# Four instead of three seven-product pairs of k-tiles in each gate/up chunk of a decoder layer

## The chip, the cores and the metric

The kernel runs on one core of a Trainium2 chip. Its time is the device time of one execution in microseconds; the median of three runs of the kernel before is 1977.46 us (1975.88 to 1978.14).

## What is computed

One decoder layer on 256 tokens of width 2048, in f32: a SwiGLU half-step, a mixing stage (a gated linear recurrence and a sparse attention behind one input projection), a cross attention on a memory of 256 tokens, a second SwiGLU half-step, and a last RMSNorm. The change touches only the two half-steps:

```
def swiglu(h, w_gate, w_up, w_down):
    return (jax.nn.silu(h @ w_gate) * (h @ w_up)) @ w_down
x = x + 0.5 * swiglu(rmsnorm(x, ffn_norm), w_gate, w_up, w_down)   # D = 2048, D_FF = 5632
```

## The kernel before, in words

**Matmuls in f32 from three passes.** Every f32 operand is split into a part hi, rounded to the type fp32r, and a rest lo. A product is three matmuls: hi by hi, hi by lo, lo by hi (`product`, L1886; `unit`, L1839). A weight unit is 512 KB. SP (the DMA queue of SyncE) loads it into one of four slots of `w_raw`; ScalarE (ACT) writes `w_hi` (L584); VectorE (DVE) writes `w_lo` = w_raw - w_hi (L1094); TensorE (PE) uses it. A load waits for the w_lo of the unit four before it (L462). w_hi of a unit waits until PE is done with the unit four before it (L583). DVE and ACT thus work four units ahead of PE (`split_ahead`, L685 and L1217: at position p they prepare the unit p + 4). Each engine takes its instructions in the order in which the program lists them.

**The gate/up stage** (`ffn_up` of each engine) makes the hidden values in 11 chunks of 512 columns. The first chunk (`opening`) is done in plain form, gate and then up, 8 units of two k-tiles each. The other ten are `body`, run as a hardware loop for chunks 1 to 9 and once more for chunk 10, with `ending` set. In a body a unit is one k-tile (128 of the 2048 rows) with 512 gate and 512 up columns, 16 units to a chunk. A plain unit (`both_unit`, L1898) makes four products, for two token halves by gate and up, into banks 0 to 3 of PSUM: 12 matmuls.

**A pair in seven-product form.** Two neighbouring units can be taken together as a product of 2 by 2 blocks with seven products instead of eight (`pair_units`, L1923): 21 matmuls instead of 24, four products in the first unit (banks 4, 6, 7, 5) and three in the second (banks 0, 1, 2). It needs sums of the blocks. The sums of tokens are made once per stage, in the opening (`token_forms` L1265, five instructions of DVE, then s_hi by ACT L715 and s_lo by DVE L1279), at the positions in FORMS_AT and FORMS_LO, in one buffer for each pair. The sums of weights are made anew in each chunk (`weight_sums`, L1235): a difference in place in w_raw (L1239), two more into `t_f32` (L1244, L1246), of which L1244 waits for both loads of the pair and, with `free_at`, until PE is done with the pair before; then t_hi by ACT (L700) and t_lo by DVE (L1229). All pairs share the one buffer t_f32, t_hi, t_lo. PAIR_AT gives the positions of the pairs in a chunk, PAIRS their k-tiles. Sums for the pair at 0 are made in the chunk before, at its position 12.

**Evictions of a chunk.** What the pairs gathered in banks 4 to 7 is added into `comb`: at MID_EV, the position of the last pair, ACT copies bank 4 (L762) and DVE adds bank 5 (L1339); at TURN_H, one position later, DVE adds banks 6 and 7 (L1343), and later bank 6 again (L1359). Also at TURN_H PE transposes the hidden values of the chunk before (`batch`, L1995, into bank 4 and 5), and ACT (L603) and DVE (L1127) split them into ffT. At position 14 DVE adds banks 0 to 3 (L1354, two instructions, behind the last unit of the chunk), ACT applies the Silu (L768), and DVE multiplies (L1288). PE begins the next chunk only when L1359 and L1127 are done (L1996, L1997).

**The down stage** (`ffn_down`) has six pairs of its own at DOWN_AT and uses the same buffers; its positions are not changed.

Of the kernel before, what the change touches and what calls it, by code (L numbers as in the profile page):

```python
# [5 lines left out]
P = 128  # L6
F32 = mybir.dt.float32
F32R = mybir.dt.float32r
# [8 lines left out]
SEQ = 256  # L17
NT = SEQ // P
# [29 lines left out]
KF = D_FF // P  # L48
# [6 lines left out]
              (C_NSA, NW), (C_NSA + NW, NW)]  # L55
             + [(c, NW) for c in (1024, 1536, 0, 512, 2048, 2560, 3072, 3584)])

PAIRS = ((0, 1), (2, 3), (4, 5))
PAIR_AT = (0, 6, 10)
W_KT = [0] * KD  # L60
for _i, _p in enumerate(PAIR_AT):
    W_KT[_p], W_KT[_p + 1] = PAIRS[_i]
_rest = [p for p in range(KD) if p not in PAIR_AT and p - 1 not in PAIR_AT]
for _kt, _p in enumerate(_rest):
    W_KT[_p] = 2 * len(PAIRS) + _kt
U_CH = KD
MID_EV = PAIR_AT[-1]
TURN_H = MID_EV + 1
NP = len(PAIRS)
DOWN_AT = (6, 12, 18, 24, 30, 36)  # L70
# [7 lines left out]
DOWN_EV = DOWN_AT[-1]  # L78
T_FFN, S_FFN = NP * (FF_CHUNKS - 1) + ND, NP + ND
EV_FFN = 3 * FF_CHUNKS + 2  # L80
FORMS_AT = ((3, 4, 11), (5, 7, 9))
FORMS_LO = ((5, 6, 14), (7, 9, 11))

U_GU1 = 0
U_DN1 = U_GU1 + 2 * U_G * FF_CHUNKS
# [65 lines left out]
def layer_program(nc, a, c, out):  # L151

    with ExitStack() as ctx:
# [8 lines left out]
        def put(name, shape, dt, size=4):  # L162
            n = size
            for s in shape[1:]:
                n *= s
            t = nc.alloc_sbuf_tensor_at(name, shape, dt, offset=at[0])
            at[0] += (n + 31) // 32 * 32
            return t
# [20 lines left out]
        s_hi = [nc.alloc_sbuf_tensor_at(f"s_hi{i}", [P, 4, P], F32R, offset=o) for i, o in enumerate(s_at)]  # L189
        s_f32 = [nc.alloc_sbuf_tensor_at(f"s_f32_{i}", [P, 4, P], F32, offset=o + 2048) for i, o in enumerate(s_at)]  # L190
        s_tmp = [nc.alloc_sbuf_tensor_at(f"s_tmp{i}", [P, 2, NT, P], F32, offset=o) for i, o in enumerate(s_at)]
        x_in = nc.alloc_sbuf_tensor_at("x_in", [P, NT, 2 * NW], F32, offset=at_xT[0])
        s_lo = [nc.alloc_sbuf_tensor_at(f"s_lo{i}", [P, 4, P], F32R, offset=o + 2048) for i, o in enumerate(s_at)]
# [26 lines left out]
        ff = at[0]  # L220
        ffT_hi = put("ffT_hi", [P, KF, SEQ], F32R)
        ffT_lo = put("ffT_lo", [P, KF, SEQ], F32R)
        ff_end = at[0]
        assert ff_end <= base + 206 * 1024, ff_end - base


# [343 lines left out]
        def _(act):  # L570
# [52 lines left out]
            def root(norm):  # L623
                act.wait_ge(var_ready, norm + 1)
                nc.scalar.activation(std[:, norm, :], var[:, norm, :], ACT.Sqrt).then_inc(std_ready, 1)
# [59 lines left out]
            def split_ahead(u0, ch, p, wide, opening=False):  # L685
# [3 lines left out]
                q = (p + SLOTS) % U_CH  # L689
                i = PAIR_AT.index(q) if q in PAIR_AT else PAIR_AT.index(q - 1) if q - 1 in PAIR_AT else None  # L690
                if not wide or i is None:
                    split(u, slot, turn_no)
                    return
                n_pair = (T_FFN if u0 else 0) + NP * ch + (1 - NP if p + SLOTS < U_CH else 1) + i
                if q in PAIR_AT:
                    act.wait_ge(t1_ready, n_pair)
# [16 lines left out]
            def token_hi(i, count):  # L713
                act.wait_ge(s_f32_ready, count)
                nc.scalar.activation(s_hi[i][:], s_f32[i][:], ACT.Copy).then_inc(s_hi_ready, 1)  # L715

            def ffn_up(u0, norm, b_h, b_x3, s_x3, base_c, base_x):
# [3 lines left out]
                def opening():  # L721
                    for k in range(2 if base_c else 0, 2 * U_G):
# [5 lines left out]
                        if not base_c and k == 10:  # L728
                            root(norm)
                        if k - 1 in FORMS_AT[u0 > 0]:  # L730
                            i = FORMS_AT[u0 > 0].index(k - 1)
                            token_hi(i, S_FFN * (u0 > 0) + i + 1)
# [349 lines left out]
        def _(dve):  # L1082
# [38 lines left out]
            def take(b, pos, lo, klo, hi, khi, scale=None):  # L1121
                dve.wait_ge(turn_hi, b + 1)
                if scale is None:
                    dyn = not isinstance(klo, int)
                    lo_v = lo[:, bass.ts(klo[0], 4), :] if dyn else lo[:, klo:klo + 4, :]
                    hi_v = hi[:, bass.ts(khi[0], 4), :] if dyn else hi[:, khi:khi + 4, :]
                    nc.vector.tensor_tensor(lo_v, turn[pos], hi_v.bitcast(F32), ALU.subtract).then_inc(turn_lo, 1)  # L1127
                    return
                for j in range(4):
                    last = nc.vector.scalar_tensor_tensor(  # L1130
                        out=lo[:, klo + j, :], in0=turn[pos][:, j, :], scalar=vec[:, scale + j:scale + j + 1],
                        in1=hi[:, khi + j, :].bitcast(F32), op0=ALU.mult, op1=ALU.subtract)
                last.then_inc(turn_lo, 1)
# [8 lines left out]
            def inverse(norm):  # L1142
                dve.wait_ge(std_ready, norm + 1)
                nc.vector.reciprocal(rstd[:, norm, :], std[:, norm, :]).then_inc(rstd_ready, 1)
                dve.wait_ge(rstd_ready, norm + 1)
# [8 lines left out]
            def split_x(j):  # L1154
                dve.wait_ge(xs_hi, j + 1)
                k = KT_U * j
                split_cols(xT_lo, k, xt_raw, k, xT_hi, k, V_F1 + k, xs_lo, KT_U)
# [59 lines left out]
            def split_ahead(u0, ch, p, wide, opening=False):  # L1217
# [3 lines left out]
                q = (p + SLOTS) % U_CH  # L1221
                i = PAIR_AT.index(q) if q in PAIR_AT else PAIR_AT.index(q - 1) if q - 1 in PAIR_AT else None
                if not wide or i is None:
# [52 lines left out]
            def token_lo(i, count):  # L1276

                dve.wait_ge(s_hi_ready, count)
                nc.vector.tensor_tensor(s_lo[i][:], s_f32[i][:], s_hi[i][:].bitcast(F32), ALU.subtract)\  # L1279
                  .then_inc(s_lo_ready, 1)  # L1280

            def ffn_up(u0, norm, b_h, b_x3, s_x3, base_c, sq):
# [3 lines left out]
                def products(up):  # L1286
                    for t in range(NT):
                        last = nc.vector.scalar_tensor_tensor(  # L1288
                            out=comb[:, 2 * t + 1, :], in0=up(t), scalar=rstd[:, norm, t:t + 1],
                            in1=comb[:, 2 * t, :], op0=ALU.mult, op1=ALU.mult)  # L1290
                    return last

                def opening():
                    for k in range(2 if base_c else 0, 2 * U_G):
                        if k == 4 and b_x3 is not None:
                            take(b_x3, 0, xT_lo, 12, xT_hi, 12, s_x3 + 12)
                        if not base_c and k < U_G - SLOTS:
                            split_x(SLOTS + k)
                        if not base_c and k == 11:
                            inverse(norm)  # L1300
                        if k == U_CH - 2:
                            dve.wait_ge(unit_done, u0 + U_CH)
                            dve.wait_ge(gate_ready, base_c + 1)
                            if b_h:
                                dve.wait_ge(turned, b_h)
                            last = products(lambda t: pair[1][:, t, :])
                            last.then_inc(h_ready, 1)
                            nc.vector.memset(taken_mark[:], 0.0).then_inc(c_taken, 2)
                        split_ahead(u0, 0, k, k + SLOTS >= U_CH, True)
                        if k in FORMS_LO[nth]:  # L1310
                            i = FORMS_LO[nth].index(k)
                            token_lo(i, S_FFN * nth + i + 1)
                        if not base_c and k in X_SQ:
                            n = X_SQ.index(k)
                            dve.wait_ge(x_loaded[n], 16)
                            link(nc.vector.scalar_tensor_tensor(
                                out=hb[:, 0, :], in0=x[:, 1, n * NW:(n + 1) * NW], scalar=1.0,
                                in1=x[:, 1, n * NW:(n + 1) * NW], op0=ALU.mult, op1=ALU.mult,
                                accum_out=ss[:, N_F1, 1, n:n + 1]))
                        if k in FORMS_AT[nth]:  # L1320
                            i = FORMS_AT[nth].index(k)
                            if i == NP - 1:
                                dve.wait_ge(sq_done, sq)
                                if base_c:
                                    dve.wait_ge(x_saved, 16)
                            if nth == 0:
                                dve.wait_ge(xs_lo, i + 1)
                            token_forms(i, PAIRS[i][0], xT_hi, xT_lo)
                        if k == (5 if base_c else 9):
                            variance(norm, sq)  # L1330
                        if base_c and k == 5:
                            inverse(norm)
# [505 lines left out]
        def _(pe):  # L1838
# [115 lines left out]
            def ffn_up(u0, b_x, b_h, b_x3, free_b, base_c):  # L1954
# [25 lines left out]
                def body(ch, ending):  # L1980
                    for p in range(U_CH):
                        u, slot = u0 + U_CH * ch + p, (u0 + p) % SLOTS
                        if p in PAIR_AT:
                            i = PAIR_AT.index(p)
                            pair_units(u, slot, i, PAIRS[i], tokens, S_FFN * nth + i + 1, T_FFN * nth + NP * (ch - 1) + i + 1,
                                       i == 0, i == NP - 1, 2 * base_c + 2 * ch if i == 0 else None)
# [520 lines left out]
```

## Time and profile before

| | |
|---|---|
| median of three runs | 1977.46 us |
| profiled execution | 1977.94 us |
| its span | 1976.1 us |
| PE busy | 1956.9 us, 99% |
| DVE busy | 1529.0 us, 77% |
| ACT busy | 1062.1 us, 54% |
| mean granted TensorE clock | 0.999 |

The span is the time from the first to the last instruction. A busy share is the mean over the whole span, with stages of different limits in it. The granted clock is a share of full speed. Durations of matmuls in the trace overlap, since they are pipelined; the distance of their starts is what one costs.

### The profile page before, as it was taken

The page shows a single profiled execution, that of the slowest core. Times are in us where ns is not written, and L with a number is a line of the kernel's source. Part 1 is how long each engine was busy: PE and PEld are TensorE (multiplying, and loading weights), DVE is VectorE, ACT ScalarE, POOL GpSimd, SP SyncE. Part 2 cuts the span into 40 slices and gives each one's busy share as a digit, 9 for nine tenths or more (in the row PEclk, how much of TensorE's full clock was granted, in tenths as well). Part 3 has the DMA queues.
Part 4 walks back from the last instruction along what each step waited for, and adds up shares of the span by engine and source line. Part 5 has one row for each costly group of instructions (what it writes and reads, how often), then busy time and mean ns, then how long its engine had stood idle before and what let it go on. Part 6 is the DMA issues. An engine that isn't in the chain of part 4 may idle for free.

```text
span 1976.1 us, 27433 instructions
## 1 busy us (share of the span) xinstructions
PE 1956.9 (99%) x10022; PEld 1616.1 (82%) x10022; DVE 1529.0 (77%) x1906; ACT 1062.1 (54%) x1305; POOL 13.6 (1%) x19
## 2 busy tenths in 40 slices
PE   9999999999999999999999999999999999999998
PEld 7888888888888888878777888888888888888886
DVE  7898899998886456766658675689999989888544
ACT  6555555555555444455555564555555555555443
POOL 0000000000000000000002000000000000000000
PEclk9999999999999999999999999999999999999999
DMA  9566666567766657565443465566666666666764
GB/s 300 184 202 199 202 193 209 183 201 235 228 222 193 194 165 220 176 198 157 137 124 114 163 202 169 160 227 207 193 191 209 187 200 205 203 208 202 247 192 147
DMA packets 148546, 382.69 MB, mean 194 GB/s; under 512 B 13424, under 2 KB 19824, under 8 KB 148080
## 3 DMA queue, kind: packets, MB, share of 16 engines
q1 hardware_dynamic: 146368, 378.70, 60.6%
q10 hardware_dynamic: 2096, 2.87, 0.4%
q8 instruction: 55, 0.90, 0.2%
q14 instruction: 27, 0.22, 0.0%
HBM read 377.33 MB, written 4.19 MB: 193 GB/s over the span
## 4 chain that ended last, share of the span: by engine, by line
PE 96%; ACT 1%; DMA 1%; DVE 1%; issue 0%; SPq 0%; DVEq 0%; ACTq 0%
PE psum L1889 54%; PE psum L1853 36%; PE psum L1876 2%; PE psum L2160 1%; PE psum L2203 1%; PE psum L1865 1%; DMA w_raw<-in_gu 0%; PE psum L2258 0%; ACT prob L886 0%; DMA w_raw<-in_w_in 0%; PE psum L2173 0%; DVE w_lo L1094 0%; ACT w_hi L584 0%; PE psum L2182 0%; ACT silu_gate L886 0%
## 5 line engine op out<-in xcount | busy, mean ns | idle before, releaser
L584 ACT ACTIVATE w_hi<-w_raw 128x1024 fp32r<-128x1024 f32 x694 | 725.7, 1056 | 674.3 <-PE psum L1853 324.7
L1094 DVE TENSOR_TENSOR w_lo<-w_raw,w_hi 128x1024 fp32r<-128x1024 f32 x694 | 835.7, 1221 | 310.1 <-ACT w_hi L584 307.9
L1889 PE MATMUL psum<-w_hi,xT_hi 128*128 128x512 f32 x920 | 360.2, 391 | 0.0
L1889 PE MATMUL psum<-w_hi,xT_lo 128*128 128x512 f32 x920 | 358.4, 390 | 0.0
L1889 PE MATMUL psum<-w_lo,xT_hi 128*128 128x512 f32 x920 | 358.3, 389 | 0.0
L1853 PE MATMUL psum<-w_hi,xT_hi 128*128 128x512 f32 (+1 forms) x544 | 213.0, 392 | 3.0 <-DVE w_lo L1211 2.8
L1853 PE MATMUL psum<-w_hi,xT_lo 128*128 128x512 f32 (+1 forms) x544 | 209.4, 385 | 0.0
L1853 PE MATMUL psum<-w_lo,xT_hi 128*128 128x512 f32 (+1 forms) x544 | 209.2, 385 | 0.0
L1889 PEld LDWEIGHTS psum<-w_hi,xT_lo 128*128 128x128 f32 x920 | 172.7, 188 | 36.1
L1889 PEld LDWEIGHTS psum<-w_lo,xT_hi 128*128 128x128 f32 x920 | 172.9, 188 | 35.1
L1889 PEld LDWEIGHTS psum<-w_hi,xT_hi 128*128 128x128 f32 x920 | 172.8, 188 | 35.1
L1853 PE MATMUL psum<-w_hi,ffT_hi 128*128 128x512 f32 x432 | 169.4, 392 | 0.0
L1853 PE MATMUL psum<-w_hi,ffT_lo 128*128 128x512 f32 x432 | 168.4, 390 | 0.0
L1853 PE MATMUL psum<-w_lo,ffT_hi 128*128 128x512 f32 x432 | 168.2, 389 | 0.0
L700 ACT ACTIVATE t_hi<-t_f 128x1536 fp32r<-128x1536 f32 x60 | 89.5, 1491 | 93.6 <-DVE t_f L1246 93.6
L1229 DVE TENSOR_TENSOR t_lo<-t_f,t_hi 128x1536 fp32r<-128x1536 f32 x60 | 105.5, 1759 | 25.3 <-ACT t_hi L700 25.3
L1853 PEld LDWEIGHTS psum<-w_hi,xT_hi 128*128 128x128 f32 x544 | 102.2, 188 | 24.1 <-DVE w_lo L1211 2.9
L1853 PEld LDWEIGHTS psum<-w_hi,xT_lo 128*128 128x128 f32 x544 | 102.1, 188 | 20.4
L1853 PEld LDWEIGHTS psum<-w_lo,xT_hi 128*128 128x128 f32 x544 | 102.4, 188 | 18.8
L1889 PE MATMUL psum<-w_hi,ffT_hi 128*128 128x512 f32 x280 | 109.5, 391 | 0.0
L1889 PE MATMUL psum<-w_lo,ffT_hi 128*128 128x512 f32 x280 | 109.1, 390 | 0.0
L1889 PE MATMUL psum<-w_hi,ffT_lo 128*128 128x512 f32 x280 | 109.1, 390 | 0.0
(319 smaller groups left out, 2508.3 us busy)
## 6 DMA issues: line engine op xcount, KB each, us to landing
w_raw<-in_gu SPq DMA_DIRECT2D x351, 512.0 KB, 4.3
w_raw<-in_d SPq DMA_DIRECT2D x176, 512.0 KB, 4.6
w_raw<-in_w_in SPq DMA_DIRECT2D x88, 512.0 KB, 3.8
w_raw<-in_w_out SPq DMA_DIRECT2D x32, 512.0 KB, 3.8
w_raw<-in_cw SPq DMA_DIRECT2D x8, 512.0 KB, 4.0
w_raw<-in_wk SPq DMA_DIRECT2D x8, 512.0 KB, 4.5
w_raw<-in_wq SPq DMA_DIRECT2D x8, 512.0 KB, 3.7
w_raw<-in_wv SPq DMA_DIRECT2D x8, 512.0 KB, 3.6
```

Source lines behind the costliest of these rows:

```text
L584: nc.scalar.activation(w_hi[:, slot], w_raw[:, slot], ACT.Copy).then_inc(w_hi_ready, 1)
L700: nc.scalar.activation(t_hi[:], t_f32[:], ACT.Copy).then_inc(t_hi_ready, 1)
L1094: nc.vector.tensor_tensor(w_lo[:, slot], w_raw[:, slot], w_hi[:, slot].bitcast(F32), ALU.subtract)\
L1229: nc.vector.tensor_tensor(t_lo[:], t_f32[:], t_hi[:].bitcast(F32), ALU.subtract).then_inc(t_lo_ready, 1)
L1853: mm = nc.tensor.matmul(dst[:, t, 0:width], act_t, w[:, slot, kk, 0:width], start=(first and kk == 0 and n == 0), stop=(last and kk == KT_ ...
L1865: mm = nc.tensor.matmul(dst[:, t, :], act_t, w[:, u % SLOTS, kk, :], start=False, stop=(last and kk == KT_U - 1 and n == 2))
L1876: tr = nc.tensor.transpose(turn[pos][:, j, t * P:(t + 1) * P], src(j, t), ident[:])
L1889: mm = nc.tensor.matmul(psum[:, bank, :], act_t, w, start=(first and n == 0), stop=(last and n == 2))
L2160: mm = nc.tensor.matmul(psum[:, 4 + hh, b * w:(b + 1) * w], qT[r, h // 2, t * P:(t + 1) * P], kT[r, b, h // REP, 0:w], start=True, stop=True)
L2203: mm = nc.tensor.matmul(psum[hh * DH:(hh + 1) * DH, 7, (r // 2) * P:(r // 2 + 1) * P], z_n[:, kk, c0:c0 + DH], probT[:, hh, (b * nk + kk) ...
```

## The change

There are four pairs, of k-tiles 0 to 7, at positions 0, 4, 8 and 12 of a chunk of 16, instead of three at 0, 6 and 10. Since MID_EV is the last pair's position, it goes from 10 to 12 and TURN_H from 11 to 13. The order of the k-tiles in a chunk (W_KT) and the count of pairs (NP) follow. A fourth buffer for the sums of tokens lies where the last four k-tiles of ffT_hi will be written in the down stage. The fourth form is made at position 12 of the opening in the first half-step and at 11 in the second, its s_lo at 15 and 13. The wait for the squares and for the saved x stays with the third form.

```diff
-PAIRS = ((0, 1), (2, 3), (4, 5))
-PAIR_AT = (0, 6, 10)
+PAIRS = ((0, 1), (2, 3), (4, 5), (6, 7))
+PAIR_AT = (0, 4, 8, 12)
...
-FORMS_AT = ((3, 4, 11), (5, 7, 9))
-FORMS_LO = ((5, 6, 14), (7, 9, 11))
+FORMS_AT = ((3, 4, 11, 12), (5, 7, 9, 11))
+FORMS_LO = ((5, 6, 14, 15), (7, 9, 11, 13))
...
+        s4_at = ff + (KF - 4) * SEQ * 4
+        s_hi.append(nc.alloc_sbuf_tensor_at("s_hi3", [P, 4, P], F32R, offset=s4_at))
+        s_f32.append(nc.alloc_sbuf_tensor_at("s_f32_3", [P, 4, P], F32, offset=s4_at + 2048))
+        s_tmp.append(nc.alloc_sbuf_tensor_at("s_tmp3", [P, 2, NT, P], F32, offset=s4_at))
+        s_lo.append(nc.alloc_sbuf_tensor_at("s_lo3", [P, 4, P], F32R, offset=s4_at + 2048))
...
-                            if i == NP - 1:
+                            if i == 2:
```

## Rows read from the trace of the kernel before

**Rows 1.** The page, part 1: busy time of each engine.

```profile
PE 1956.9 (99%) x10022; PEld 1616.1 (82%) x10022; DVE 1529.0 (77%) x1906; ACT 1062.1 (54%) x1305; POOL 13.6 (1%) x19
```

**Rows 2.** The page, part 4: the chain of waits by line.

```profile
PE psum L1889 54%; PE psum L1853 36%; PE psum L1876 2%; PE psum L2160 1%; PE psum L2203 1%; PE psum L1865 1%; DMA w_raw<-in_gu 0%; PE psum L2258 0%; ACT prob L886 0%; DMA w_raw<-in_w_in 0%; PE psum L2173 0%; DVE w_lo L1094 0%; ACT w_hi L584 0%; PE psum L2182 0%; ACT silu_gate L886 0%
```

**Rows 3.** Stretch view of one chunk: length, busy time and instructions by engine, clock, DMA.

```profile
212.94:255.34 42.40, 42.40 (x193) 35.19 (x192) 38.33 (x36) 23.56 (x24) 0.00 (x0) 1.00 0.62 198
```

**Rows 4.** Order of time, PE: start, us, line, operation, count.

```profile
54.04 0.39 PE L1889 MATMUL psum<-w_hi,xT_hi 128*128 128x512 f32 x1
...
201.59 0.39 PE L1889 MATMUL psum<-w_hi,xT_hi 128*128 128x512 f32 x1
...
211.80 1.04 PE L1876 MATMUL psum<-ident,comb 128*128 128x128 f32 x8
```

**Rows 5.** Order of time, DVE, from a chunk's end into the next.

```profile
216.35 0.68 DVE L1359 TENSOR_TENSOR comb<-psum,comb 128x512 f32<-128x512 f32 x1
216.95 0.68 DVE L1239 TENSOR_TENSOR w_raw<-w_raw 128x512 f32<-128x512 f32 x1
217.66 0.69 DVE L1244 TENSOR_TENSOR t_f<-w_raw 128x512 f32<-128x512 f32 x1
218.39 1.23 DVE L1246 TENSOR_TENSOR t_f<-w_raw,t_f 128x1024 f32<-128x1024 f32 x1
219.53 1.22 DVE L1094 TENSOR_TENSOR w_lo<-w_raw,w_hi 128x1024 fp32r<-128x1024 f32 x1
221.17 1.76 DVE L1229 TENSOR_TENSOR t_lo<-t_f,t_hi 128x1536 fp32r<-128x1536 f32 x1 [0.42 <-ACT t_hi L700]
222.85 1.22 DVE L1094 TENSOR_TENSOR w_lo<-w_raw,w_hi 128x1024 fp32r<-128x1024 f32 x1
223.98 2.35 DVE L1354 TENSOR_TENSOR comb<-psum,comb 128x1024 f32<-128x1024 f32 x2
226.25 2.35 DVE L1094 TENSOR_TENSOR w_lo<-w_raw,w_hi 128x1024 fp32r<-128x1024 f32 x2
228.52 1.41 DVE L1288 SCALAR_TENSOR_TENSOR comb<-comb,rstd 128x512 f32<-128x512 f32 x2
229.84 2.35 DVE L1094 TENSOR_TENSOR w_lo<-w_raw,w_hi 128x1024 fp32r<-128x1024 f32 x2
...
233.24 0.69 DVE L1244 TENSOR_TENSOR t_f<-w_raw 128x512 f32<-128x512 f32 x1 [0.44 <-DMA w_raw<-in_gu]
```

**Rows 6.** Groups by line, DVE, of that chunk: count, busy us, mean ns, idle before.

```profile
L1094 DVE TENSOR_TENSOR w_lo<-w_raw,w_hi 128x1024 fp32r<-128x1024 f32 x16 | 19.0, 1219 | 0.2 <-ACT w_hi L584 0.2
...
L1244 DVE TENSOR_TENSOR t_f<-w_raw 128x512 f32<-128x512 f32 x3 | 2.1, 692 | 2.2 <-PE psum L1889 1.7 <-DMA w_raw<-in_gu 0.4
```

**Rows 7.** A w_lo behind a t_lo, the load it frees, landings of two loads.

```profile
196.41 3.49 DVE L1094 TENSOR_TENSOR w_lo<-w_raw,w_hi 128x1024 fp32r<-128x1024 f32 x3
...
L463 SPq DMA_DIRECT2D w_raw<-in_gu x1: 333/333/333, 197.8 to 197.8; - x1
DMA to landing us min/median/max: 3.5/3.5/3.5
...
DMA to landing us min/median/max: 4.9/4.9/4.9
```

**Rows 8.** Order of time, DVE: a token form, and ends of both openings.

```profile
30.12 0.68 DVE L1267 TENSOR_TENSOR s_tmp<-xT_hi,xT_lo 128x512 f32<-128x512 f32 x1
...
31.90 1.22 DVE L1094 TENSOR_TENSOR w_lo<-w_raw,w_hi 128x1024 fp32r<-128x1024 f32 x1
...
50.49 1.22 DVE L1094 TENSOR_TENSOR w_lo<-w_raw,w_hi 128x1024 fp32r<-128x1024 f32 x1
...
1306.43 1.22 DVE L1094 TENSOR_TENSOR w_lo<-w_raw,w_hi 128x1024 fp32r<-128x1024 f32 x1
1308.27 1.41 DVE L1288 SCALAR_TENSOR_TENSOR comb<-psum,rstd,comb 128x512 f32<-128x512 f32 x2 [0.62 <-PE psum L1853]
```

**Rows 9.** Stretch view of the opening of the first half-step.

```profile
10.00:13.00 3.00, 0.52 (x3) 0.39 (x3) 1.67 (x4) 2.18 (x5) 0.00 (x0) 1.00 1.05 373
```

## Prediction

> **What bounds the kernel now.** I read the busy line of the page first [rows 1]: TensorE (PE) works 99% of the span, VectorE (DVE) 77%. The chain of waits [rows 2] says the same: 54% of the span is PE at L1889, the products of the two feed-forward (FFN) stages, and no other engine has more than 1%. The stretch view of one gate/up chunk [rows 3] shows what these averages hide. In a chunk of 42.40 us PE is busy for all 42.40, but DVE for 38.33, so the chunk has one engine that is full and another that is 90% full. The change lightens the first and loads the second, so the question is how much room DVE really has.
>
> A chunk is 16 units. A plain unit is 12 matmuls of 128x512, a pair of units in seven-product form 21 instead of 24. From the first matmul of unit 8 to the transposes behind unit 11 stand 24 + 21 = 45 matmuls in 211.80 - 201.59 = 10.21 us [rows 4]: 0.227 us each. So PE takes 183 x 0.227 + 1.04 (8 transposes) = 42.6, which is the period.
>
> **DVE's queue for a chunk**, by start-to-start distances of instructions that did not wait [rows 5]:
> - w_lo, 16 per chunk [rows 6]: 2.27 / 2 = 1.135 each, 18.16.
> - The evictions: L1359 0.60 and L1339, of the same shape, as much; L1343 and L1127, of w_lo's shape, 1.135 each; the two L1354 2.27, the two L1288 1.32. Together 7.06.
> - A pair's sums: L1239 0.71, L1244 0.73, L1246 1.14, L1229 1.68. Between L1246 and L1229 stands one w_lo, and t_lo cannot start before ScalarE (ACT) has made t_hi: L1229 starts 2.78 us after L1246, that is 2.78 - 1.14 - 1.135 = 0.505 more than the queue alone. Together 4.765.
>
> Three pairs: 18.16 + 7.06 + 14.30 = 39.52. The other 2.88 of the 42.40 are waits: 1.7 for PE and 0.4 for a load at L1244 [rows 6], the rest small ones around the evictions.
>
> **The change part by part.** *PE* loses 3 matmuls in each of 20 chunks (ten per FFN go through the loop body): 60 x 0.227 = 13.6 us. Its chunk becomes 180 x 0.227 + 1.04 = 41.9.
>
> *DVE* gets 4.765 more per chunk and has 2.88 of slack: 39.52 + 4.765 = 44.28, above PE's 41.9. From here DVE sets the period, and each of its waits counts in full. Three terms come on top or go:
>
> (a) The reload. L1244 needs the unit behind the pair's first. Its slot is free when the w_lo four units earlier is done. That w_lo now stands directly behind the t_lo of the pair before, and only two w_lo and one L1239 stand between it and L1244: naive distance 3 x 1.135 + 0.71 = 4.12. A load is issued 1.35 after the start of its w_lo (196.41, issue at 197.76) and the first of a burst lands after 3.5, the next one after 4.9 [rows 7]. I take 3.5, since the load in question is again the first behind a t_lo: 1.35 + 3.5 + 0.15 = 5.0 (0.15 for the signal is an estimate: at 233.24 L1244 starts 5.86 after the w_lo at 226.25 + 1.135 that freed its load, which leaves 0 to 1 between those landings). That is a wait of 0.88 at the pairs at 8 and 12, and 0.3 at the next chunk's pair at 0, where L1339 (0.60) lies between. With 4.9 it would be 2.3, 2.3 and 1.7; with none, zero. The pair at 4 has the evictions between.
>
> (b) The evictions are issued at positions 12 and 13, so at 13 L1343 now stands between the w_lo and t_lo and fills the 0.505: minus 0.5.
>
> (c) L1244 of the next chunk's pair 0 stands at 12 and waits for unit 13 (the t buffers). Unit 12's 12 matmuls and 13's 9 end at 35.7 in the walk below, L1244 is due at 36.9: no wait.
>
> The walk, from the start of the first L1354 (0): w_lo 2, 3 at 2.3, 3.4; L1288 4.5; sums of pair 4 from 5.86, t_lo 10.1, w_lo 5 11.8; sums of 8 from 15.2, L1244 at 16.8 after its wait, t_lo 20.3, w_lo 9 22.0; sums of 12 from 25.4, L1244 26.95, t_lo 30.5, w_lo 13 to 15 32.1 to 34.4; L1339 35.55; L1239 36.15, L1244 37.1, L1246 37.9, w_lo 39.0, L1343 40.15, t_lo 41.3, w_lo 43.0, L1127 44.1, L1359 45.23; next L1354 at 45.83. That is 44.28 + 0.88 + 0.88 + 0.29 - 0.505. PE beside it: starts at 0.2, 2.72 for a plain unit and 4.76 for a pair, is through unit 5 at 15.3, unit 9 at 25.5, unit 13 at 35.7, waits for L1339 to transpose (37.4), ends unit 15 at 42.8, and then stands until L1359 is done, 3.1 us. Before, four plain units (10.9 us) lay between the transposes and the chunk's end and hid these evictions; now two do (5.4 us).
>
> ACT gets one t_hi of 1.5 us and moves its copy and its take; it is busy about 24 of 42 us and meets no due time in the walk. SP issues the same 16 loads per chunk in the same order of slots (other k-tiles in them), each behind the w_lo that frees its slot, so they spread with DVE; GpSimd issues nothing here.
>
> *Ends.* Chunks 2 to 9 of each FFN: 45.83 - 42.40 = 3.43 each, 16 of them: 54.9. In chunk 10 no sums for a next chunk stand: DVE is free in time and PE needs 42.6, +0.2, twice: 0.4. Chunk 1 inherits the fourth token form made in the opening: 1.78 (30.12 to 31.90) [rows 8] and 0.60 for its s_lo. In FFN1 the w_lo of unit 16 is at 50.49; then form 1.78, t_lo 1.68, four w_lo (17 to 19 and 16's own, 4.54), L1288 1.32, two s_lo 1.2: L1239 at 61.0, which is 7.0 behind PE's first matmul (54.04) [rows 4] where the steady chunk has 5.7. So 3.4 + 1.3 = 4.7. In FFN2 w_lo 17 moves from 1306.43 to 1308.2; three w_lo with it, s_lo, L1288: L1239 at 1313.5, 5.3 behind PE (1308.27) [rows 8]: 3.43 - 0.35 = 3.1. The down stages keep their sums; at their entry DVE is again ahead of PE: zero.
>
> Sum: 54.9 + 0.4 + 4.7 + 3.1 = 63.1. The profiled execution took 1977.94 (span 1976.1), the median of the runs is 1977.46, 0.5 less, so I leave it out: **2041 us, 3.2% slower**. PE's 13.6 us are inside the periods.
>
> **The rivals.**
> 1. *No reload wait* (loads land before L1244): period 43.78, +1.38 in 16 chunks, chunks 1 at 2.6 and 1.0, +0.4: about +26, 2004. For it: loads may land sooner once DVE spaces them wider. Against: L1244 already waits 0.44 for a load at 233.24, after a longer distance. 12%.
> 2. *The clock falls in the new stall.* PE stands 3.1 us per chunk. In the trace its longest stand is in the stretch 10 to 13 us, 0.52 busy of 3, and the granted clock there is 1.00 [rows 9], so 2.4 GHz; a stand of 3 us is not shown. If it came back at 1.2 GHz, the first pair's 21 matmuls would take up to 9.5 instead of 4.8, and L1244 of pair 4, due 6.4 behind PE's start, would wait up to 3.1: up to +56 over 18 chunks; 2060 to 2097. Together with loads that land after 4.9 (up to +4.2 in a chunk, 2115) 11%.
> 3. *Faster, as the matmuls alone say*: 1977.94 - 13.6 = 1964. This needs DVE to fit 4.77 into 2.88. Taking all waits as removable, DVE's busy time alone is 38.33 + 0.69 + 0.69 + 1.23 + 1.76 = 42.7 [rows 3, 5], still above 42.40. Only shorter instructions could do it: 3%. No change (within 0.2%, 4 us, which is about what a measurement here can tell) would need the same in part: 2%. The rest, 72%, is the forecast, 2027 to 2055.
>
> For the second rival the Trainium skill, "TensorE: Matmul & The Clock Gate", section "HAM oscillation", describes a kernel whose waits for data let the clock drop again and again, each time paid at the restart; by it the second rival would be the outcome, 2060 or more. No stand of this length is in the trace of before, and the row on 10 to 13 us speaks the other way for a slightly shorter one.
>
> **Range and chances.** 2003 to 2066 takes in the first rival, the forecast and the low end of the second; its own range alone is 2027 to 2055. Slower 0.95, same 0.02, faster 0.03.
>
> **What would show it.** Period of L1343 to L1343 in the loop near 45.8. DVE above 90% busy there, PE near 41.9 of 45.8, with one idle of about 3 us per chunk before L1889, released by DVE L1359. L1244 waiting about 0.9 for a load twice per chunk and never long for PE. t_lo at 13 without its 0.42 idle. First chunk of FFN1 longer than the others by about 1. Down and middle stages unchanged. The forecast is wrong if the period stays at 42, if the granted clock leaves 1.0, or if the L1244 waits are 0 or above 2.

## The result and the profile after

The changed kernel takes 2064.15 us (median of four runs, 2063.52 to 2065.75) beside 1977.45 for the kernel before in the same comparison: ratio 1.0442 (95% interval 1.0429 to 1.0454), 4.4% slower. The profiled execution took 2064.32 us, its span is 2062.5. The forecast said 2041. The time lies 23 us above it and inside the range given (2003 to 2066), but that range took in the low end of the second rival: it is outside the forecast's own 2027 to 2055 and inside the second rival's 2060 to 2097.

The changed kernel has five lines more near its top, so each line number in its trace is 5 higher than before: L1348 is L1343 of before, L1359 is L1354, L1364 is L1359, L1249 is L1244.

The page after, part 1, which answers to [rows 1]: PE has 60 matmuls fewer and 86 us more span to do the rest in; DVE has 85 us more work.

```profile
PE 1977.1 (96%) x9962; PEld 1620.6 (79%) x9962; DVE 1613.9 (78%) x1998; ACT 1086.5 (53%) x1327; POOL 13.6 (1%) x19
```

The chain of waits by engine (part 4) was 96% PE before; now PE has 61% of it and DVE, the loads and ACT have 30%.

```profile
PE 61%; DVE 14%; DMA 10%; issue 8%; ACT 6%; DVEq 0%; SPq 0%; ACTq 0%
```

The waits, summed over the span (who waited for whom: us in total, times, longest). The first line had no counterpart before; a chunk's first matmul now waits at 18 chunk starts, 3.5 us on average. The last two are the load and PE waits of the second sum of weights.

```profile
PE psum L1894 <- DVE comb L1364: 63.5, 18, 3.9
...
DVE t_f L1249 <- DMA w_raw<-in_gu: 37.0, 45, 2.3
...
DVE t_f L1249 <- PE psum L1894: 25.3, 25, 1.8
```

The stretch view of one chunk after, from one L1348 to the next, answers to [rows 3]: 46.81 us instead of 42.40, DVE busy 42.43 instead of 38.33, and the granted clock at 0.96.

```profile
236.06:282.87 46.81, 43.53 (x189) 35.68 (x188) 42.43 (x41) 24.79 (x25) 0.00 (x0) 0.96 0.56 179
```

The same chunk on DVE, in order of time (start, us, line, and in brackets the idle time ahead and what ended it). The evictions L1348 to L1359 follow one another without a gap, with t_lo, one w_lo and L1132 between them. The four L1249 wait 0.79 and 0.97 for PE, then 0.88 and 0.22 for a load.

```profile
236.06 1.22 DVE L1348 TENSOR_TENSOR comb<-psum,comb 128x1024 f32<-128x1024 f32 x1
237.20 1.75 DVE L1234 TENSOR_TENSOR t_lo<-t_f,t_hi 128x1536 fp32r<-128x1536 f32 x1
238.86 1.22 DVE L1099 TENSOR_TENSOR w_lo<-w_raw,w_hi 128x1024 fp32r<-128x1024 f32 x1
240.00 1.22 DVE L1132 TENSOR_TENSOR ffT_lo<-psum,ffT_hi 128x1024 f32 x1
241.13 0.68 DVE L1364 TENSOR_TENSOR comb<-psum,comb 128x512 f32<-128x512 f32 x1
241.85 2.35 DVE L1359 TENSOR_TENSOR comb<-psum,comb 128x1024 f32<-128x1024 f32 x2
...
249.19 0.69 DVE L1249 TENSOR_TENSOR t_f<-w_raw 128x512 f32<-128x512 f32 x1 [0.79 <-PE psum L1894]
...
259.43 0.69 DVE L1249 TENSOR_TENSOR t_f<-w_raw 128x512 f32<-128x512 f32 x1 [0.97 <-PE psum L1894]
...
269.58 0.69 DVE L1249 TENSOR_TENSOR t_f<-w_raw 128x512 f32<-128x512 f32 x1 [0.88 <-DMA w_raw<-in_gu]
...
279.87 0.69 DVE L1249 TENSOR_TENSOR t_f<-w_raw 128x512 f32<-128x512 f32 x1 [0.22 <-DMA w_raw<-in_gu]
```

PE at the start of this chunk, in order of time. It stands 3.28 us until L1364 is done (241.13 + 0.68 = 241.81, and 0.62 more until the first matmul). The first five starts are followed by distances of 0.23 to 0.31, the next eight by 0.39 to 0.43, and from 247.08 on it is 0.23 again.

```profile
238.76 0.39 PE L1894 MATMUL psum<-w_hi,xT_lo 128*128 128x512 f32 x1
242.43 0.47 PE L1894 MATMUL psum<-w_hi,xT_hi 128*128 128x512 f32 x1 [3.28 <-DVE comb L1364]
...
243.43 0.48 PE L1894 MATMUL psum<-w_lo,s_hi 128*128 128x512 f32 x1
243.71 0.63 PE L1894 MATMUL psum<-w_hi,s_lo 128*128 128x512 f32 x1
244.13 0.63 PE L1894 MATMUL psum<-t_hi,s_hi 128*128 128x512 f32 x1
...
247.08 0.40 PE L1894 MATMUL psum<-w_lo,xT_hi 128*128 128x512 f32 x1
247.31 0.39 PE L1894 MATMUL psum<-w_hi,xT_lo 128*128 128x512 f32 x1
```

The stretch view names the reason: the granted clock (the column behind POOL) is 0.50, the 1.2 GHz level, and full again by 248.00.

```profile
244.00:246.00 2.00, 2.00 (x6) 1.52 (x6) 2.00 (x3) 0.72 (x1) 0.00 (x0) 0.50 0.00 0
...
248.00:250.00 2.00, 2.00 (x10) 1.69 (x9) 1.18 (x3) 1.06 (x1) 0.00 (x0) 1.00 0.87 338
```

**Where the 87 us are.** By the traces, the first gate/up stage is 41.3 us longer (forecast 32.3), the second 46.5 (30.7), the work between the first down stage's start and the second opening 1.2 shorter, and the second down stage as before, to 0.2 (from PE's first matmuls: down stage 477.94 and 519.19, second opening 1269.10 and 1309.16, second down stage 1731.97 and 1818.56). The periods of chunks 2 to 9, from one L1348 to the next, are 46.87, 46.15, 46.85, 46.81, 47.76, 45.99, 46.75, 45.96 in the first stage and 48.02, 47.26, 48.00, 46.46, 47.07, 47.21, 47.24, 47.02 in the second. Four of the sixteen have a granted clock of 1.00 (46.15, 45.99, 45.96, 46.46); nine are at 0.96 and three at 0.93.

### The profile page after: what moved, and what is told of

Read it like the earlier page. It is cut to its first block, busy times and chain, and to the rows that moved or that the text cites. A ratio compares the mean times of both kernels' runs of the same rounds, so it can differ in the third digit from the quotient of the medians.

```text
span 2062.5 us, 27521 instructions
## 1 busy us (share of the span) xinstructions
PE 1977.1 (96%) x9962; PEld 1620.6 (79%) x9962; DVE 1613.9 (78%) x1998; ACT 1086.5 (53%) x1327; POOL 13.6 (1%) x19
## 4 chain that ended last, share of the span: by engine, by line
PE 61%; DVE 14%; DMA 10%; issue 8%; ACT 6%; DVEq 0%; SPq 0%; ACTq 0%
PE psum L1858 33%; PE psum L1894 23%; DMA w_raw<-in_gu 9%; DVE w_lo L1099 5%; ACT t_hi L705 3%; DVE t_f L1251 2%; ACT w_hi L589 2%; DVE t_f L1249 2%; DVE t_lo L1234 1%; DVE ffT_lo L1132 1%; PE psum L1881 1%; PE psum L2165 1%; PE psum L2208 1%; DVE comb L1364 1%; PE psum L1870 1%
## 5 line engine op out<-in xcount | busy, mean ns | idle before, releaser
L1894 PE MATMUL psum<-w_hi,xT_hi 128*128 128x512 f32 x800 | 317.7, 397 | 65.4 <-DVE comb L1364 63.5
L1894 PE MATMUL psum<-w_lo,xT_hi 128*128 128x512 f32 x800 | 313.8, 392 | 0.0
L1894 PE MATMUL psum<-w_hi,xT_lo 128*128 128x512 f32 x800 | 313.7, 392 | 0.0
L1894 PEld LDWEIGHTS psum<-w_hi,xT_hi 128*128 128x128 f32 x800 | 151.9, 190 | 104.0 <-issue 70.6
L705 ACT ACTIVATE t_hi<-t_f 128x1536 fp32r<-128x1536 f32 x80 | 119.4, 1492 | 122.6 <-DVE t_f L1251 122.6
L1894 PEld LDWEIGHTS psum<-w_hi,xT_lo 128*128 128x128 f32 x800 | 151.6, 190 | 32.1
L1894 PEld LDWEIGHTS psum<-w_lo,xT_hi 128*128 128x128 f32 x800 | 151.8, 190 | 30.2
L1858 PE MATMUL psum<-w_hi,ffT_lo 128*128 128x512 f32 x432 | 168.2, 389 | 0.0
L1858 PE MATMUL psum<-w_lo,ffT_hi 128*128 128x512 f32 x432 | 168.1, 389 | 0.0
L1234 DVE TENSOR_TENSOR t_lo<-t_f,t_hi 128x1536 fp32r<-128x1536 f32 x80 | 140.5, 1757 | 25.7 <-ACT t_hi L705 25.7
L1858 PEld LDWEIGHTS psum<-w_lo,xT_hi 128*128 128x128 f32 x544 | 102.3, 188 | 19.0
L1251 DVE TENSOR_TENSOR t_f<-w_raw,t_f 128x1024 f32<-128x1024 f32 x92 | 112.7, 1225 | 3.1
L1249 DVE TENSOR_TENSOR t_f<-w_raw 128x512 f32<-128x512 f32 x92 | 63.7, 693 | 65.4 <-DMA w_raw<-in_gu 37.0
L1894 PE MATMUL psum<-w_hi,ffT_hi 128*128 128x512 f32 x280 | 109.3, 390 | 0.3 <-DVE comb L1359 0.2
```

The costliest lines, as they stand in the source:

```text
L705: nc.scalar.activation(t_hi[:], t_f32[:], ACT.Copy).then_inc(t_hi_ready, 1)
L1234: nc.vector.tensor_tensor(t_lo[:], t_f32[:], t_hi[:].bitcast(F32), ALU.subtract).then_inc(t_lo_ready, 1)
L1249: nc.vector.tensor_tensor(t_f32[:, 2, :], b22, b12, ALU.subtract).then_inc(t2_ready, 1)
L1251: nc.vector.tensor_tensor(t_f32[:, 0:2, :], w_raw[:, slot:slot + 2, 0, :], t_f32[:, 2, :].unsqueeze(1).broadcast_to([P, 2, NW]), ALU.subtr ...
L1858: mm = nc.tensor.matmul(dst[:, t, 0:width], act_t, w[:, slot, kk, 0:width], start=(first and kk == 0 and n == 0), stop=(last and kk == KT_ ...
L1894: mm = nc.tensor.matmul(psum[:, bank, :], act_t, w, start=(first and n == 0), stop=(last and n == 2))
```

## The experiments

Two theories were put against each other. A: DVE's queue is full, and its total with the load waits is the period (this is how the prediction adds up). B: the period is set by one chain per chunk, from the end of unit 12 through the evictions to PE's restart; it would be there with three pairs as well. Beside them stood the question of what the clock takes. All ratios are to the kernel before on the same chip, 1977.11 us in the first four and 1976.57 in the last three.

**Three pairs, with the evictions where the change puts them.** The kernel before with

```diff
-PAIR_AT = (0, 6, 10)
+PAIR_AT = (0, 6, 12)
```

> Three pairs as before, but at 0, 6 and 12, so that the evictions stand at 12 and 13 as in the changed kernel; DVE has no added work (39.5 us of queue against PE's 42.4 per chunk). Theory A, my prediction's (DVE's queue total sets the period): nothing is over PE's time, 1977 to 1985. Theory B (the chain from the end of unit 12 to L1359 sets it, whatever the queue holds): unit 12 ends 34.0 behind PE's start of the chunk, L1339 at 35.0, then L1239, L1244, L1246, a w_lo, L1343, t_lo, a w_lo, L1127, L1359, 10.1 us, so PE starts the next chunk at about 45: +2.5 in 18 chunks, 2022. PE would stand about 2.5 us per chunk; at full clock if that is short enough.

Measured: 2063.47 us (2062.00 to 2064.97), ratio 1.0436 (1.0419 to 1.0454), the same as the change with all its sums. A is out for this kernel, and B's 2022 was too low as well: the period at full clock is 45.8 to 45.9 and not 45, and in 13 of the 16 chunks the clock fell, which made them 47.4 to 47.5. The stretch view shows a chunk in which DVE is busy for no more than before, 38.50 of 45.82 us:

```profile
282.38:328.20 45.82, 42.65 (x193) 35.06 (x192) 38.50 (x37) 23.88 (x24) 0.00 (x0) 1.00 0.60 183
```

The lines of before are valid here. ACT's copy waits until unit 12 is done, which is when its last t product ends, at 323.03, and from there every piece follows the one ahead of it:

```profile
323.06 0.60 ACT L762 ACTIVATE comb<-psum 128x512 f32<-128x512 f32 x1 [1.66 <-PE psum L1889]
...
323.76 0.69 DVE L1339 TENSOR_TENSOR comb<-psum,comb 128x512 f32<-128x512 f32 x1 [1.10 <-ACT comb L762]
324.37 0.68 DVE L1239 TENSOR_TENSOR w_raw<-w_raw 128x512 f32<-128x512 f32 x1
...
328.20 1.22 DVE L1343 TENSOR_TENSOR comb<-psum,comb 128x1024 f32<-128x1024 f32 x1
329.34 1.75 DVE L1229 TENSOR_TENSOR t_lo<-t_f,t_hi 128x1536 fp32r<-128x1536 f32 x1
...
333.27 0.68 DVE L1359 TENSOR_TENSOR comb<-psum,comb 128x512 f32<-128x512 f32 x1
...
334.57 0.59 PE L1889 MATMUL psum<-w_hi,xT_hi 128*128 128x512 f32 x1 [3.13 <-DVE comb L1359]
```

That is 11.5 us, of which PE has work for 8.4, until 331.44 (334.57 - 3.13). In the kernel before, the matmul that ended the first unit of the last pair, and the chunk's last one, were these (order of time, PE):

```profile
209.52 0.39 PE L1889 MATMUL psum<-t_hi,s_lo 128*128 128x512 f32 x1
...
223.37 0.39 PE L1889 MATMUL psum<-w_hi,xT_lo 128*128 128x512 f32 x1
```

From 209.91 to the end of L1359 at 217.03 [rows 5] are 7.1 us, 7.7 with the restart, under 13.8 us of work. So the move took 5.4 us of cover away, and it made the chain 3.8 longer, because at position 12 the sums for the next chunk's first pair, and at 13 its t_lo, are now listed between L1339 and L1359. Against these 9.2 us stood 6.1 of slack: 3.1 remain, the stall. B is right on this: the evictions' place alone costs the whole 86 us, without any fourth pair, some 21 of them by way of the clock (13 chunks at 1.6).

**Four pairs, but the sums of the pair at 4 cut to 8 of 512 columns** (left out: the rest of these sums), which takes 3.6 us per chunk of DVE's busy time away (42.43 to 38.83) and leaves most of the chain.

```diff
-                nc.vector.tensor_tensor(b12, b12, w_raw[:, slot, 0, :], ALU.subtract).then_inc(t1_ready, 1)
+                nc.vector.tensor_tensor(b12, b12, w_raw[:, slot, 0, 0:c], ALU.subtract).then_inc(t1_ready, 1)
...
+                            None if opening else u0 + U_CH * ch + PAIR_AT[i - 1] + 2, 8 if i == 1 else NW)
```

> The changed kernel, but the weight sums of the pair at 4 (L1239, L1244, L1246, t_hi, t_lo) are made for 8 columns of 512 in the loop chunks, which leaves that part of the result out. DVE loses about 3.9 us per chunk and stands at about 40.4, under PE's 41.9. Theory A: PE sets the period, 1964 to 1970. Theory B: unit 12 ends at 33.5, L1339 at 34.5, the same chain behind it, period about 44.6, 2019. With a clock that falls in the stall up to 15 more.

Measured: 2057.37 us (2049.39 to 2059.89), ratio 1.0398 (1.0373 to 1.0424). The four runs are 10 us apart, so the gain of 7 us is known only roughly; the periods say more. At full clock they are 45.1 to 45.6, some 0.9 below the change; DVE now idles, 1.9 us for PE in one place. A, by which more than 3 us per chunk should go, falls as the only bound. B said 2019, with up to 15 more for the clock; its chain stands at 45.1 to 45.6 instead of 44.6, and the change's 46.0 to 46.5 is DVE's queue on top.

**The stall filled.** The change, with twelve matmuls that nothing uses, into a free bank, between the chunk's last unit and the wait for L1364.

```diff
+                    if not ending:
+                        pe.wait_ge(combined, EV_FFN * nth + 3 * ch - 1)
+                        for _ in range(12):
+                            nc.tensor.matmul(psum[:, 7, :], ...)
```

> The changed kernel with 12 matmuls of 128x512 that nothing reads, into bank 7 once L1343 has freed it, at the end of each chunk but the last, while PE would stand. Nothing else is moved. If the granted clock falls because PE stands 3.2 to 3.9 us, it stays at 1.00 now and every period is that of the chunks that kept their clock, 46.0 in the first FFN and 46.4 in the second: about 13 us less, 2051. If the clock is no cause, 2064 or more.

Measured: 2049.48 us (2047.39 to 2050.11), ratio 1.0363 (1.0346 to 1.0381), 14.7 us less than the change, with the same dependences and more work for PE. The clock is 1.00 in every chunk, PE's idle time before the restart 0.9 to 1.3, the periods 45.9 to 46.4. One restart and one chunk of it:

```profile
241.32 0.47 PE L1894 MATMUL psum<-w_hi,xT_hi 128*128 128x512 f32 x1 [0.96 <-DVE comb L1364]
...
234.95:280.87 45.92, 44.96 (x202) 36.75 (x201) 42.33 (x42) 24.54 (x25) 0.00 (x0) 1.00 0.57 183
```

So 14.7 us of the 87 are the clock. The trace of the change says the same in another way: behind the 14 restarts at which the clock fell, the sums of the pair at 4 waited for PE (the 0.79 at 249.19 is one such wait; three of the others in chunks 2 to 9 are 1.7 to 1.8), 15.0 us in all, and behind the four others they did not wait.

**The evictions first.** The change, with position 13 listed in another order: L1348, w_lo, L1364 and L1132, and only then t_lo and its w_lo (ACT takes ffT ahead of t_hi).

```diff
+                            split(u0 + U_CH * ch + MID_EV + SLOTS, (u0 + MID_EV) % SLOTS)
+                            dve.wait_ge(combined, base_e + 3 * ch - 1)
+                            nc.vector.tensor_tensor(comb[:, 3, :], psum[:, 6, :], comb[:, 2, :], ALU.add).then_inc(combined, 1)
+                            take(b_h - 1 + ch, 0, ffT_lo, (ch - 1,), ffT_hi, (ch - 1,))
...
+                        split_ahead(u0, ch, p, not (ending and p + SLOTS >= U_CH), late=p == MID_EV)
```

> The changed kernel with DVE's order at position 13 changed: L1343, w_lo, L1359, L1127, then t_lo and w_lo of the next pair, and ACT's take ahead of its t_hi. DVE's work is the same. PE's stall of 3.2 us at the end of the chunk should break into pieces under 1.5 us (L1127 is done 43.1 behind the first L1354, unit 15 at 42.8), so the clock stays. Theory A: DVE's queue still sets 45.8 to 46.4 per chunk: 2048. Theory B: the chain to L1359 is 3 us shorter and the period falls below 44, under 2010.

Measured: 2048.93 us (2047.19 to 2050.05), ratio 1.0364 (1.0347 to 1.0382). PE's stand is down to 1.09 us, and behind L1132:

```profile
237.76 0.47 PE L1896 MATMUL psum<-w_hi,xT_hi 128*128 128x512 f32 x1 [1.09 <-DVE ffT_lo L1132]
```

The clock stays at 1.00, but the period does not move below 45.7 to 46.3: the 2 us that PE gets at the chunk's start it gives back in small waits for DVE (L1365, which here adds banks 0 to 3, w_lo, t_lo).

```profile
232.95:278.66 45.71, 43.25 (x189) 34.08 (x188) 42.25 (x41) 24.66 (x24) 0.00 (x0) 1.00 0.58 182
```

Here A is right: with the chain shortened, DVE's queue holds the period where it was. The gain of 15 us is the clock's, as in the filled kernel.

**Three pairs with the evictions first.** The kernel above with `PAIRS` and `PAIR_AT = (0, 6, 12)`.

> Three pairs at 0, 6 and 12 (as e1_three_at_12) with the order of e4_evict_first at position 13. If what e1 showed is the chain from unit 12 to L1359 and L1127, it is now about 3 us shorter: unit 12 ends 34.3 behind PE's start, L1127 8 us later, and with 0.6 us until PE goes on again the period is 43.0 to 44.0: 1988 to 2006. If the late place of the evictions costs by itself, in whatever order, it stays above 2040.

Measured: 2006.56 us (2006.37 to 2007.96), ratio 1.0152 (1.0136 to 1.0169); period 43.9, DVE busy 38.3 of it:

```profile
222.57:266.48 43.91, 43.19 (x193) 34.95 (x192) 38.32 (x37) 23.50 (x24) 0.00 (x0) 1.00 0.60 191
```

Beside the first experiment this prices the order of one position: 2063.47 to 2006.56, 57 us (56 by the ratios), some 21 of them the clock's. Beside the one before it prices the fourth pair, once the chain is short: 42 us, 2.0 per chunk. What is left to the kernel before is 1.5 us per chunk. In one chunk I added up the starts of PE's matmuls that are more than 0.26 apart: 1.5 us beyond the usual distance, 1.04 of it at the chunk's first matmul (0.60) and at the first one of the pair's second unit (0.44), which waits for the evictions at the chunk's end, and about 0.1 at each of five more; before, 0.1 in all.

**Four pairs, evictions first, and the narrow sums** (left out: the same as above).

> The four pairs with both loads taken off: the order of e4_evict_first and the narrow sums of e2_narrow_sums (pair at 4 for 8 of 512 columns, that part of the result left out). e2 alone took 7 us off and e4 alone 15. If two bounds lie side by side (DVE's queue at 46.0 and the chain behind unit 12 at 45.2), taking both gives far more than the sum: period 42.8 to 43.5, 1985 to 1998. If something else holds 45, it is 2040 or more.

Measured: 2007.14 us (2005.02 to 2008.48), ratio 1.0153 (1.0136 to 1.0169); 1985 to 1998 was expected, so it gained less than thought. The freed time came back in part as load waits: in the waits of the whole span, L1253 (L1249 of the change) now has the largest sum of the four-pair kernels.

```profile
DVE t_f L1253 <- DMA w_raw<-in_gu: 60.4, 56, 2.0
```

Yet the two edits together take off 57 us, singly 7 and 15. The periods at full clock show it without the clock's share: 46.0 to 46.5 with neither edit, 45.1 to 45.6 and 45.7 to 46.3 with one of them, 43.7 to 44.3 with both. That is how two bounds side by side show themselves: removing either leaves the other.

```profile
223.43:267.30 43.87, 42.73 (x191) 34.55 (x190) 38.65 (x42) 23.39 (x24) 0.00 (x0) 1.00 0.59 193
```

**The load wait by itself.** Evictions first, and the load of each pair's second unit cut from 512 KB to 128 KB (left out: the rest of those columns, which stay stale).

```diff
-                        load(u0 + U_CH * ch + p, (u0 + p) % SLOTS, both(w, W_KT[p], ch))
+                        src = both(w, W_KT[p], ch)
+                        load(u0 + U_CH * ch + p, (u0 + p) % SLOTS, src[:, :, 0:128] if p - 1 in PAIR_AT else src)
```

> e4_evict_first, but the load of each pair's second unit brings 128 of 512 rows' columns in each half of the chunk's weights (128 KB instead of 512 KB), the rest of that unit stays old: that part of the result is left out. The waits of L1249 for a load (0.95, 0.95 and 0.4 us in each chunk) should go or shrink to 0.3 and less. Theory A says that each counts in full: 1.7 to 2.2 us in 18 chunks, 2010 to 2019. If the waits are hidden beside something else, 2045 or more.

Measured: 2023.66 us (2023.11 to 2026.37), ratio 1.0241 (1.0224 to 1.0258); every period is 44.8 instead of 45.7 to 46.3. The loads' waits are gone, but at the pair at 12 a wait for PE stands in their place (on this kernel's DVE, L1251 is the L1249 of the change):

```profile
258.68 0.69 DVE L1251 TENSOR_TENSOR t_f<-w_raw 128x512 f32<-128x512 f32 x1 [0.67 <-PE psum L1897]
```

So the loads are worth 24 us by the ratios, 0.9 to 1.5 per chunk, not the 2.2 or so of their waits; my expectation of 2010 to 2019 had counted them nearly whole. In the trace of the changed kernel the wait is a plain chain (the chain of waits in order of time): the w_lo that frees the slot, SP's issue, 3.51 us of load, the sum.

```profile
264.62 1.23 DVE w_lo L1099
...
265.94 0.03 SPq L468
...
266.00 3.51 DMA w_raw<-in_gu
...
269.58 0.70 DVE t_f L1249
```

## Why the prediction came out as it did

**The range held by luck.** Two things went another way than the forecast said: the clock fell, which the prediction itself had named as a sign that it is wrong, and the bound is not DVE's queue alone. With the clock's 14.7 us off, the time is the 2049 of the filled stall, inside the forecast's own 2027 to 2055.

**The period.** 45.83 was forecast, and the four chunks of full clock took 45.96 to 46.46. In PE's sum of 42.6 the transposes stand with their duration, 1.04; from their start to that of the next matmul are 0.79 (211.80 to 212.59), which makes 42.3. The walk held in its places: the stall stands before L1894 and ends with L1364, t_lo at position 13 lost its 0.42 of idle, and the first difference in place of chunk 1 (L1239 before, L1244 now) started at 60.38 (walk: 61.0).

**(a) The reload waits** were forecast as 0.88, 0.88 and 0.29; in the four chunks of full clock they are 0.9 to 1.2, 0.8 to 1.0 and 0.4 to 0.5, all for a load. Where the clock fell, the first of them is in part put down to PE, and the pair at 4 waited for PE besides, which "never long for PE" had excluded. The landing of 3.5 [rows 7] was the right one of the two candidates; here it is 3.51. Rival 1, no such wait, is out. Nor would a missing wait have brought the period from 45.83 to that rival's 43.78, 2.05 less: with short loads it is 44.8, 0.9 to 1.5 less.

**"From here DVE sets the period"** is the step whose reason fell short. It is true in the change by less than 1 us. The chain from unit 12 to L1364 holds the period at 45.1 to 45.9 by itself; with three pairs DVE is idle beside it for 7 us per chunk. The walk had both in it, and its end, "then stands until L1359 is done, 3.1 us", is the measured stall (3.1 to 3.9). But the sum booked everything to the fourth pair's 4.765, although moving MID_EV and TURN_H past the next pair's sums would have cost as much alone. The chain could have been priced from the same rows, if roughly: the expectation of the first experiment did so and came to a period of 45, where 45.8 to 45.9 were measured (11.5 us over 8.4 us of work).

**The restart** was taken as 0.2 us behind L1359 and is 0.62. At full clock that, and slightly longer load waits, are the 0.1 to 0.6 us by which periods exceed the forecast, some 5 us over sixteen chunks; how the two share it was not taken apart.

**The clock** is the term that was mis-sized: zero in the forecast, 14.7 us by the filled stall. Rival 2 had the mechanism (the stall, the 1.2 GHz level at the restart, the wait of pair 4 for PE) with 11% and an end of up to +56; the slow stretch covered seven to nine matmuls as a rule, eleven to thirteen at four restarts, and not the 21 of a pair, so it cost 0.8 to 1.8 us a time. (Its upper end with late loads is 2117 by its own terms, 2041 + 18 x 4.2, not 2115.) Its argument against, [rows 9], was weak: 0.52 us busy in three at an unchanged clock lay in another stage, with matmuls inside it. The Trainium skill, "TensorE: Matmul & The Clock Gate", section "HAM oscillation", describes a matmul kernel whose waits for data let the clock drop at each turn of a loop, each time paid at the restart. The trace agrees on the drop, 0.50 granted from 244.00 to 246.00 behind a stand of 3.28 us, but not on its coming each time. In the three-pair kernel three of the sixteen chunks, behind stands of 3.17, 3.24 and 3.26, kept 1.00 and took 45.8 to 45.9; the others, behind 3.13 to 3.27, took 47.4 to 47.5. The length of the stand doesn't separate them: there the clock fell even behind 2.93 us, at the start of chunk 10 (the first line), and in the change it stayed behind 3.50 (the second):

```profile
476.62 0.47 PE L1889 MATMUL psum<-w_hi,xT_hi 128*128 128x512 f32 x1 [2.93 <-DVE comb L1359]
...
1538.92 0.47 PE L1894 MATMUL psum<-w_hi,xT_hi 128*128 128x512 f32 x1 [3.50 <-DVE comb L1364]
```

What the three-pair trace does show is a drift: at the starts of chunks 2 to 5 of the first stage 1, 2, 4 and 6 distances between matmuls are at full speed before the first slow one, at chunk 6 none is slow, and at chunks 7 to 10 it is 0, 2, 4 and 6. What decides is open.

**Chunks 1 and 10 and the openings** were forecast at +8.2 and came to about +13.6 (the two stages' 87.8 less 39.1 and 33.9 in chunks 2 to 9, less the 1.2). In chunk 1 one load wait was 2.35 us instead of 0.88, at 82.90, and at the start of chunk 10 the clock fell in both stages. Together: 18 us in chunks 2 to 9 and 5 at their ends make the 23.

**Not reached.** No kernel here beats the one before. With PE full for 42.40 us [rows 3], a fourth pair can bring at most 0.68 us per chunk, some 14 in all, and it needs both the chain under PE's work and at least 2.4 of the 44.28 us of DVE's queue somewhere else (44.28 less 41.9). Giving the sums to GpSimd, which is busy 1% of the time, was not tried.

## What to carry to other kernels

Before adding up an engine's queue, follow one chain: from the producer's last instruction to the release of the buffer that the bottleneck needs next, through the program's order, and compare it with the work that covers it. A due time that is moved past other work of the same engine costs twice, the cover lost and the work that now stands in the chain. When two bounds lie within 1 us of each other, an experiment that removes one shows almost nothing (here 7 us, and 15 that were the clock's, against 57 for both), so remove both once before judging either. A PE stall of 3 us can have a second price at its restart; the kernels here whose stalls in each chunk were about 1.3 us or less never paid it.

## What the runs showed of the hardware

- Behind a stand of 3.28 us the first five matmuls still started at full speed, and only then, 1.3 us after the restart, eight were 0.43 apart; in the three-pair kernel, behind 3.13, the starts were 0.38 and then 0.43 apart from the restart on.
- Behind stands from 2.93 to 4.08 us the granted clock fell at most restarts, and behind others from 2.93 to 3.50 it did not (the change, the three-pair kernel and the narrow sums). All kernels whose longest regular stand in a chunk was about 1.3 us or less held 1.00, and so did the kernel before behind its single stand of 2.48 us, which ended at 12.56.
- DVE done to PE's first matmul is 0.62 us (241.81 to 242.43; 333.95 to 334.57).
- A 512 KB load landed 3.51 us after its issue when it was the first behind a pause (266.00 in the change), the same as before [rows 7].
